# A two-block transformer kernel: 64 tokens of the expert stage computed from rows fetched by indirect DMA, the dense products 448 wide, query and key norms on ScalarE

## What is computed

```python
def one_block(hx):
    q = (hx @ w_q).reshape(TOKEN_BLOCK, PEER_HEADS, 2, PEER_HALF)
    s = jnp.einsum('nhpd,hpkd->nhpk', q, sub_keys).astype(jnp.float32)
    top_s, top_i = lax.top_k(s, PEER_TOPK)
    cand = top_s[:, :, 0, :, None] + top_s[:, :, 1, None, :]
    best_s, best_p = lax.top_k(cand.reshape(TOKEN_BLOCK, PEER_HEADS, PEER_TOPK * PEER_TOPK), PEER_TOPK)
    ...
    gate = jax.nn.softmax(best_s, axis=-1).reshape(TOKEN_BLOCK, PEER_HEADS * PEER_TOPK).astype(hx.dtype)
    u_sel = u[expert]
    v_sel = v[expert]
    act = jax.nn.gelu(jnp.einsum('nd,ned->ne', hx, u_sel), approximate=False)
    return jnp.einsum('ne,ned->nd', gate * act, v_sel)
```

## Time and profile before

| | |
|---|---|
| median of 3 runs | 2605.48 us |
| the profiled execution | 2603.68 us, its span 2601.9 us |
| TensorE matmul busy | 2467.9 us, 95% of the span |
| VectorE, ScalarE, GpSimd busy | 54%, 22%, 60% |
| TensorE clock granted, mean | 0.98 of full |
| DMA | 375.41 MB, mean 144 GB/s |

### The profile page before, as it was taken

How to read it: one execution, slowest core, us unless ns; L and a number is a source line. 1 busy time by engine, 2 the same in 40 slices (tenths; PEclk the granted TensorE clock), 3 DMA queues, 4 the chain that set the end, 5 groups by cost and what they waited for, 6 DMA issues and landing times.

```text
span 2601.9 us, 37796 instructions
## 1 busy us (share of the span) xinstructions
PE 2467.9 (95%) x12856; PEld 1258.8 (48%) x12856; DVE 1405.7 (54%) x2431; ACT 585.3 (22%) x1194; POOL 1559.2 (60%) x1048
## 2 busy tenths in 40 slices
PE   6879989999999999999999999999899898999997
PEld 3435534444555555434444444444357544457743
DVE  6996748998677777229722222240204533564434
ACT  2112211111222222111111111110126332245412
POOL 6764459888766766799866666560570166830063
PEclk8989999999999999999999999999999999999999
DMA  6224443555447857877755655560220022210021
GB/s 261 92 79 156 142 164 122 149 154 150 141 147 237 257 153 238 264 258 269 247 203 200 206 198 208 198 217 13 82 97 1 9 89 89 97 49 1 9 73 49
DMA packets 189247, 375.41 MB, mean 144 GB/s; under 512 B 13536, under 2 KB 79200, under 8 KB 189152
## 3 DMA queue, kind: packets, MB, share of 16 engines
q1 hardware_dynamic: 119696, 332.64, 38.2%
q10 hardware_dynamic: 69456, 41.50, 5.4%
HBM read 302.78 MB, written 71.30 MB: 144 GB/s over the span
## 4 chain that ended last, share of the span: by engine, by line
PE 83%; POOL 2%; DVE 2%; issue 1%; ACT 1%; DMA 0%; DVEq 0%; SPq 0%; POOLq 0%; ACTq 0%
PE ps L683 68%; PE ps L820 4%; PE ps L841 4%; PE ps L829 2%; PE ps L953 2%; PE ps L764 1%; POOL arena L653 1%; POOL parts L635 1%; DVE ps L1337 1%; ACT arena L1091 0%; POOL ring L633 0%; POOL arena L651 0%; DVE arena L1370 0%; PE ps L812 0%; PE ps L1053 0%
## 5 line engine op out<-in xcount | busy, mean ns | idle before, releaser
L683 PE MATMUL ps<-hT,parts 128*128 128x512 f16 x4800 | 1055.8, 380 | 38.2 <-DVE arena L1371 14.1
L632 POOL TENSOR_SCALAR parts<-ring 128x1024 f16<-128x1024 f32 x261 | 289.0, 1107 | 809.4 <-PE ps L683 784.1
L683 PEld LDWEIGHTS ps<-hT,parts 128*128 128x128 f16 x4800 | 467.0, 98 | 597.7 <-issue 22.3
L683 PE MATMUL ps<-arena 128*128 128x512 f16 x3072 | 667.4, 380 | 6.7 <-DVE arena L1734 6.7
L635 POOL TENSOR_TENSOR parts<-ring,parts 128x1024 f16<-128x1024 f32 x261 | 568.8, 2179 | 21.8
L683 PEld LDWEIGHTS ps<-arena 128*128 128x128 f16 x3072 | 301.2, 98 | 373.7 <-issue 14.8
L1729 DVE TENSOR_TENSOR arena<-arena 128x512 f32<-128x512 f32 x128 | 143.6, 1122 | 432.7 <-DMA arena<-gate_mem 430.2
L653 POOL TENSOR_TENSOR arena<-ring,arena 128x1024 f16<-128x1024 f32 x128 | 283.0, 2211 | 10.7
L633 POOL TENSOR_SCALAR ring<-ring 128x1024 f32<-128x1024 f32 x261 | 282.0, 1081 | 0.0
L651 POOL TENSOR_SCALAR arena<-ring 128x1024 f16<-128x1024 f32 x128 | 147.7, 1154 | 170.3 <-PE ps L683 170.3
L1202 ACT ACTIVATE spare<-ps 128x512 f32<-128x512 f32 x128 | 76.5, 597 | 567.5 <-PE ps L683 419.2
(11 more groups left out here) (172 smaller groups left out, 2270.2 us busy)
## 6 DMA issues: line engine op xcount, KB each, us to landing
ring<-w SPq DMA_DIRECT2D x133, 512.0 KB, 3.3
ring<-u SPq DMA_DIRECT2D x128, 512.0 KB, 3.9
ring<-v SPq DMA_DIRECT2D x128, 512.0 KB, 3.4
act_mem<-spare SPq DMA_DIRECT2D x128, 256.0 KB, 4.0
gate_mem<-arena ACTq DMA_DIRECT2D x4, 8192.0 KB, 42.7
arena<-act_mem SPq DMA_DIRECT2D x128, 256.0 KB, 3.6
arena<-gate_mem SPq DMA_DIRECT2D x128, 256.0 KB, 3.9
arena<-ada_w SPq DMA_DIRECT2D x48, 512.0 KB, 6.4
```

What stands on the lines that cost most here:

```text
L632: G.tensor_scalar(dst[:, 0, :], src, WS, 1.0, ALU.mult, ALU.mult).then_inc(scaled, 1)
L683: ins = [T.matmul(out_, a, b, start=start and j == 0, stop=stop and j == 2) for j, (a, b) in enumerate(((lhs[0], rhs[0]), (lhs[0], rhs[1]) ...
```

## The change

`FEW` = 64: the last 64 tokens leave the dense stage. `DENSE` = 448 tokens stay: up and down matmuls, gelu, `act_mem`, `gate_mem`, pairs and products are 448 wide; gates are spread in 56 groups (chunks 48 to 103), stored as 4 batches of 112 tokens (runs of 448 B). For the 64 tokens, expert numbers and gates go through a small HBM buffer (`pick_mem`) and come back with the 128 picks divided over two sides: partition 64h + n, column k holds pick 64h + k of token n. So one indirect DMA fetches 128 rows of 4 KB of `u` (or `v`), one per partition, into one of 4 buffers, and 64 of them make a pass. TensorE transposes the 64 tokens' features (32 matmuls), VectorE takes 64 dot products of 128x1024 with them out of PSUM, ScalarE applies gelu, and in the down stage VectorE adds 64 weighted rows of `v`; 8 fp32 matmuls with `fold` add the two sides.

GpSimd issues the fetches: 4 at chunk 56, then 3 ahead of each tile from chunk 108 on, then one at about every 1.75 chunks of the down stage. For tiles 108 to 127 of `u`, ScalarE does the first two of the three cutting operations. In the norms ScalarE squares out of PSUM and scales the keys and two of four query blocks; the gains are applied when the transposed rows are copied.

```diff
+            def cut_raised(n):
+                pool.wait_ge(raised, 2 * (n - T_EXP - RAISED + 1))
+                src, dst = ring[:, n % RING, :], parts[:, n % RING, :, :]
+                G.tensor_tensor(dst[:, 1, :], src, dst[:, 0, :], ALU.subtract).then_inc(parts_ready, 1)
+            def fetch(n):
+                if n >= ROWS_AHEAD:
+                    wait_apart(rows_used, n - ROWS_AHEAD + 1)
...
+                G.indirect_dma_start(
+                    out=fetched_rows[:, n % ROWS_AHEAD, :], out_offset=None, in_=rows,
...
-            cut_tiles(RING, T_TWO, 0)
+            cut_tiles(RING, T_EXP + FETCH, 0)
+            pool.wait_ge(pick_loaded, 16 * 2 * SIDES)
+            for n in range(ROWS_AHEAD):
+                fetch(n)
+            cut_tiles(T_EXP + FETCH, T_EXP + RAISED, 0)
+            n = ROWS_AHEAD
+            for c in range(RAISED, CHUNKS):
+                for _ in range(3):
+                    if n < FEW:
+                        fetch(n)
+                        n += 1
+                cut_raised(T_EXP + c)
+            while n < FEW + ROWS_AHEAD:
+                fetch(n)
+                n += 1
...
+            for c in range(CHUNKS):
+                while n < 2 * FEW and few_chunk(n - FEW) <= c:
+                    fetch(n)
+                    n += 1
                 cut_v(c)
...
-            ups(AT_GATES + 4, AT_GATES + S // GROUP, 4)
-            ups(AT_GATES + S // GROUP, CHUNKS)
+            ups(AT_GATES + 4, AT_GATES + GROUPS, 4)
+            for k in range(KC):
+                for side in range(SIDES):
+                    for j, half in enumerate(hr(k)):
+                        mm = T.matmul(ps[side * FEW:(side + 1) * FEW, 4 + k // 4, (k % 4) * P:(k % 4 + 1) * P],
+                                      half[:, DENSE:S], ident_h, start=(j == 0), stop=(j == 1))
+            mm.then_inc(few_turned, 1)
+            ups(AT_GATES + GROUPS, CHUNKS)
...
+            pe.wait_ge(rows_used, FEW)
...
+            for c in range(AT_GATES + GROUPS, CHUNKS):
+                gelu_chunk(c % 4, c)
+                if RAISED <= c + RING - 1 < CHUNKS:
+                    raise_tile(T_EXP + c + RING - 1)
...
+            for k in range(FEW):
+                row = await_rows(k)
+                V.tensor_tensor_reduce(out=row, in0=row, in1=few_h, scale=1.0, scalar=0.0, op0=ALU.mult,
+                                       op1=ALU.add, accum_out=few_dot[:, k:k + 1]).then_inc(rows_used, 1)
...
+                    V.scalar_tensor_tensor(out=few_sum, in0=row, scalar=w, in1=few_sum, op0=ALU.mult,
+                                           op1=ALU.add).then_inc(rows_used, 1)
```

```diff
-            take("q", lambda s, b: copy(tq[:, s, :], b))
-            take("kvi", lambda s, b: copy(tr[:, s, :], b[:, 0:KVI]))
+            for i in range(NT):
...
+                own.do(A.activation(mask[:, i, :], b, ACT.Square, scale=1.0 / WS), q_squares)
+                own.do(copy(tq[:, i, :], b), took["act"])
+            for i in range(NT):
...
+                for j, a in enumerate((0, 2 * HD)):
+                    own.do(A.activation(dup[:, j, i, 0:HD], b[:, a:a + HD], ACT.Square, scale=1.0 / WS,
+                                        accum_out=stat[:, i * 10 + 8 + j:i * 10 + 9 + j]))
+                own.do(copy(tr[:, i, :], b[:, 0:KVI]), took["act"])
...
+            for i in range(2, NT):
+                for h in range(HEADS):
+                    own.do(A.activation(tq[:, i, h * HD:(h + 1) * HD], tq[:, i, h * HD:(h + 1) * HD], ACT.Copy,
+                                        scale=stat2[:, i * 10 + h:i * 10 + h + 1]), tok_scaled)
```

More of the change, by code:

```diff
@@ L906, in _ @@
             features("up_attn", in_parts(oT), lambda k: pe.wait_ge(turned_read, 6 + k + 1))
-            features("out", in_parts(gT), lambda k: pe.wait_ge(tok_ready, 3 + k + 1), behind(1, 2))
+            features("out", in_parts(gT), lambda k: pe.wait_ge(tok_ready, 2 + k + 1), behind(1, 2))
             last_parts(1, 2)
@@ L938, in up @@
                 for k in range(KC):
-                    first, last = three(ps[:, r % 2, :], piece(T_EXP + r, k * P, P), hr(k), k == 0, k == KC - 1)
+                    hi, lo = hr(k)
+                    first, last = three(ps[:, r % 2, 0:DENSE], piece(T_EXP + r, k * P, P),
+                                        (hi[:, 0:DENSE], lo[:, 0:DENSE]), k == 0, k == KC - 1)
                     if k == 0:
@@ L992, in down_chunk @@
                     lhs, rhs = down_parts(at, o)
-                    first, last = three(ps[:, o, :], lhs, rhs, isinstance(c, int) and c == 0, False)
+                    first, last = three(ps[:, o, 0:DENSE], lhs, rhs, isinstance(c, int) and c == 0, False)
                 last.then_inc(down, 1)
@@ L1007, in _ @@
                     lhs, rhs = down_parts(c % (2 * GROUP), o)
-                    first, last = three(ps[:, o, :], lhs, rhs, False, c == CHUNKS - 1)
-                last.then_inc(down, 1)
+                    three(ps[:, o, 0:DENSE], lhs, rhs, False, c == CHUNKS - 1)
+                T.matmul(ps[:, o, DENSE:S], few_sum[:, o * P:(o + 1) * P], fold, start=True,
+                         stop=True).then_inc(down, 1)
                 if o >= 2:
@@ L1483, in _ @@
-            for i in range(NT):
-                dve.wait_ge(took["act"], count_taken("kvi", i))
-                own.do(V.tensor_tensor(scr[:, 0, 0:HD], tr[:, i, 0:HD], tr[:, i, 0:HD], ALU.mult))
-                own.link(V.tensor_tensor(scr[:, 0, HD:2 * HD], tr[:, i, 2 * HD:3 * HD], tr[:, i, 2 * HD:3 * HD], ALU.mult))
-                own.link(V.tensor_reduce(stat[:, i * 10 + 8:i * 10 + 10],
-                                         scr[:, 0, 0:2 * HD].rearrange("p (h d) -> p h d", d=HD), AX, ALU.add),
-                         stat_ready if i == NT - 1 else None)
@@ L1490, in _ @@
-            dve.wait_ge(root_ready, 1)
-            own.link(V.reciprocal(stat2[:, 0:40], stat2[:, 0:40]))
-            for i in range(NT):
+                dve.wait_ge(q_squares, i + 1)
+                own.do(V.tensor_reduce(stat[:, i * 10:i * 10 + 8], mask[:, i, :].rearrange("p (h d) -> p h d", d=HD),
+                                       AX, ALU.add), stat_ready if i == NT - 1 else None)
+            dve.wait_ge(root_ready, 1)
+            own.link(V.reciprocal(stat2[:, 0:40], stat2[:, 0:40]), rates)
@@ L1500, in _ @@
[L1500 to L1507 removed]
+                own.do(V.tensor_tensor(q3, q3, rs, ALU.mult), tok_ready)
```

221 lines of the change are left out of this document (149 added, 72 removed).

## The result

The changed kernel takes 2667.14 us (median of 4 runs, 2665.37 to 2671.51) against 2605.57 for the kernel before on the same chip: ratio 1.024, 95% interval 1.0228 to 1.0252. It is **slower by 61.6 us**; 2511 was forecast, with a range of 2470 to 2575.

A forecast was written before the change was run, and what follows sets the result against it. TensorE was taken as the bound, with DMA bounding the fetch phase and GpSimd the down stage after the change. Terms summed to -94.4 us from 2603.7, 2509.3, plus 1.8 for the median: 2511 us, range 2470 to 2575.

The forecast's parts named there:

- Norms: Start of the kernel: squares moved to ScalarE remove TensorE's wait for VectorE before the transposes, -3.4 us.
- Chunks 0 to 43: First up chunks: TensorE saves 11.1 us, then waits about 17 us for VectorE's gates; the exponentials wait for nothing new.
- The restart: Matmuls after TensorE's wait behind chunk 43 run partly at the lower clock level, +1.7 us.
- turning: Before the fetches: 32 TensorE matmuls that turn the 64 tokens' features, +2.1 us.
- folding: Down stage: eight fp32 matmuls adding the two sides, some 0.25 us each, +2 us.
- fetch phase: Chunk 104 to the end of up: DMA-bound at 400 GB/s, +34.9 us of waiting, +12.2 with narrower matmuls and fewer gates.
- the slower rival: Fetch phase and down: GpSimd's fetch costs more than 1.0 us; at 1.98 the whole gain is gone; 10%.
- Short runs: Gate stores: runs of 448 B might cost twice as much as 512 B, +40 us, 2551 us; 18%.
- The step that failed: Fetch phase: ScalarE's raising of tiles, some 2.2 us a chunk beside a gelu of 0.6, is hidden.
- signs of being wrong: Gate stage over 5.5 us a group, a fetch keeping GpSimd far from 1 us, or a fetch phase not DMA-bound.
- The down stage: Down chunks: GpSimd, busy 4.76 us a chunk, bounds the stage instead of TensorE at 4.545, -59.0 us.
- pause: Change from up to down: GpSimd's four fetches and cut take some 5 us, costing about what it did.

The follow-up runs named there:

- Experiment 1: Changed kernel with SyncE issuing each activation store before the load of a later tile, chunks 96 to 127: 2586.11 us (one run).
- 3: Changed kernel with GpSimd doing all three cutting operations and ScalarE no longer raising tiles, fetches kept: 2611.03 us (one run).
- 2: Changed kernel with 60 of the 64 fetches of `u` left out, dot products and ScalarE's raising kept: 2636.56 us (one run).
- experiment 4: Changed kernel with GpSimd issuing each fetch of `v` rows three chunks later in the down stage: 2625.54 us (one run).
- 5: Changed kernel with SyncE loading each chunk's pair ahead of the tile of `v` in the down stage: 2629.89 us (one run).
- kernel 6: Changed kernel with both SyncE's stores before loads (chunks 96 to 127) and `v` fetches three chunks later: 2545.45 us (median of 5), ratio 0.9775 to the kernel before.

## Why the prediction was wrong

**What held, and what held in part.** Norms: TensorE's products ended at 87.4, with 88.7 forecast (the kvi product moved the next one by 1.94 us, from 64.72 to 66.66, not by 3.1), the 6.52 us of wait went, and so did a restart that took 24 transposes 4.51 us instead of 2.78: the up stage starts 5.3 us earlier, 3.4 forecast. Chunks 0 to 43: -13.5 us against -14.5. The wait of some 17 us came, 16.1 of it, but in another place: 14.12 stand ahead of chunk 42, because ScalarE sat at the exponentials, 18.5 us, until VectorE's picks were there at 622.1, as before, with two gelus behind it. Before the change ScalarE came to the exponentials at 634.6 and waited for nothing. So "wait for nothing new" was right of their input and wrong of ScalarE, and what stood behind that wait was not followed: the same omission as below, here at no price. Gates: the period is 5.43 us as forecast. The restart cost 1.4 of 1.7 (24.04 us for five chunks, 22.68 at full speed), turning 1.0 of 2.1, folding 1.4 of 2.0 (no row stood behind its 0.25 us a matmul; it took 0.17, from 1852.78 to 1852.95). A fetch costs GpSimd 0.94 us in the fetch phase, 1.0 forecast: the slower rival, which needed 1.98, fell, and the kernel was slower for a reason that no case had.

**Short runs, a rival with 18%.** The four gate stores of the changed kernel are not alike. The second and third landed after 48.4 and 48.0 us, the first and last after 35.5 and 37.6; the four of before, 512 B a run, after 41.8 to 43.1. What the DMA engines were busy with them (packets, MB, share of 60 us from the issue), first the second store of before (870.6:930.6), then the first and second of the changed kernel (737.5:797.5 and 813.6:873.6):

```profile
q10 hardware_dynamic: 16400, 8.39, 48.7%
q10 hardware_dynamic: 16400, 7.34, 43.6%
q10 hardware_dynamic: 16400, 7.34, 56.8%
```

The third's share is 57.3%, the last's 43.4%. So a run of 448 B cost some 17% more than one of 512 B in two of the stores, and 10% less in the other two, which is near its part of the bytes. The stores differ in where in a row of 1792 B they begin (0, 448, 896, 1344 B); that this is the cause was not tried. Twice as much, as the rival had it, no store cost, and TensorE had no idle time in the gate stage; so the rival fell, but it was not without a ground. The Trainium skill has it, in DMA: Bandwidth & Descriptors, section "Specifications", that below 512 B a transfer is done as read-modify-write; the trace agrees for two stores of four, with a third more for each byte, and shows no such cost in the other two.

**The step that failed.** "Raising tiles on ScalarE, some 2.2 us a chunk beside a gelu of 0.6, is hidden too", with "GpSimd's share of a chunk is three fetches and 2.12 us". Both sums are right, as loads: ScalarE is busy 24.33 us of 114. Neither is a path. The raising was added to ScalarE's order behind a gelu, GpSimd's cut was made to wait for the raising, SyncE's load waits for the cut, the store is queued behind the load, and the next gelu but one waits for the store. The forecast asked how much each engine does in a chunk, and never followed what is queued behind each new wait; SyncE's queue, whose order was not changed, does not occur in that step at all. Price: 107.6 us where 12.2 were forecast, 95.4 too many. Experiment 1 cuts this loop at the store and 3 at the raising, and they give back 81 and 56 us; 2 takes the load off the DMA engines and leaves the loop, and gives back 31. One of the forecast's own signs of being wrong, a fetch phase not bound by DMA, is what came.

**The down stage.** "GpSimd: ... = 4.76 us" comes close to what the stage costs once its loop is cut, 4.81 measured. What was missed is the same thing again. GpSimd's fetch was taken as one microsecond of work and not as a wait for VectorE's row buffer, with the cutting behind it, the tile's load behind that, and VectorE's own pair behind the load. Price: -4.8 us in place of -57.

That 4.76 and 4.81 lie so near is in part luck. In experiment 4 the cutting took 3.68 us of GpSimd and the fetch 0.95, where 4.19 and 0.57 were forecast, and VectorE, "2.0 of 4.8, covered", had no slack. Over the same window (1460 to 1590 us) of experiments 4, 5 and 6 GpSimd was busy 124.93, 123.26 and 124.73 us of 130, and VectorE 128.91, 118.39 and 123.00, at 4.81 to 4.83 us a chunk each time: GpSimd's load is the steady one, as forecast, but part of it is time behind VectorE, and no experiment parts the two.

**What was off in size.** Kernel 6 has both loops cut and is the one to hold the sum against. It stands at 2545.5, 34.5 over the forecast, the result of three terms:

| stretch | kernel 6, us | change from before | forecast |
|---|---|---|---|
| to chunk 104 | 966.93 | -48.4 | -49.6 |
| fetch phase | 153.9 | +22.2 | +12.2 |
| pause | 15.7 | +13.2 | 0 |
| down | 628.5 | -46.4 | -57.0 |
| the rest | 777.8 | +0.3 | 0 |

Fetch phase: with the DMA engines full it moved 366 GB/s, not the 400 that the forecast took between 421 and 370 (kernel 6):

```profile
1005.00:1110.00 105.00, 84.13 (x375) 38.84 (x374) 57.09 (x93) 38.09 (x47) 75.61 (x62) 0.89 1.00 366
```

By that rate the forecast's 53.9 MB take 147.3 us instead of 134.7, 12.6 more; 10.0 are missing. Down: once in step, at 4.8 us a chunk, it is as forecast, but it starts badly, with a second pause of 7.54 us at 1160 for VectorE. The pause between up and down, 15.7 us where "some 5 us", as before, were forecast, is a third case of SyncE's order. Its timeline in kernel 6:

```profile
1119.11 1.06 POOL L706 TENSOR_SCALAR arena<-ring 128x1024 f16<-128x1024 f32 x1
...
1122.39 0.34 SPq L556 DMA_DIRECT2D ring<-v  x1
...
1127.03 0.42 SPq L607 DMA_DIRECT2D act_mem<-spare  x1
...
1132.52 0.54 ACT L1306 ACTIVATE spare<-ps 128x448 f32<-128x448 f32 x1 [12.70 <-DMA act_mem<-spare]
```

GpSimd cuts the first tiles of `v` only after four fetches of its rows, each of which waits for a dot product; the load of `v` waits for the cut; four pairs follow it; and the third last store of `act_mem` goes out behind them all at 1127.03, while the last gelu waits 12.70 us for stores. That this is worth mending was not tried.

## What to carry to other kernels

Beside the sum of each engine's work for one chunk, write down the cycle: from each new wait to what is queued behind it on the same engine or DMA queue, to who waits for that, until it closes; the longest cycle is the price, and it can be twice the largest load (experiment 2: 9.1 us, where the fullest engine, TensorE, had 4.54). When a window shows no resource near 1 and TensorE idle, look for such a cycle, and first at a queue where a transfer that frees something stands behind one that waits. Swapping two issues on SyncE was worth 81 us here, as much as the narrower products save in 125 chunks.

## What was not expected of the hardware

- **Stretched operations.** In experiment 4's down stage VectorE's 128x448 product (L1858) took 1.90 us on average, where its shortest took 0.61, and the sum over 128x1024 (L1870) 3.15, where its shortest in the changed kernel took 1.27. GpSimd's two operations went from 1.04 to 1.30 and from 2.12 to 2.38. In kernel 6 the second of these took 2.72 and VectorE's other product (L1856) 2.10: who pays differs from run to run. The Trainium skill says in SBUF — State Buffer, section "SBUF: two separate sides", that a VectorE operation with two SBUF inputs and a GpSimd operation that reads SBUF exclude each other for the whole instruction, whichever started first. The traces agree; two rows of kernel 6:

```profile
1501.36 2.98 POOL L708 TENSOR_TENSOR arena<-ring,arena 128x1024 f16<-128x1024 f32 x1
1502.28 2.54 DVE L1856 TENSOR_TENSOR arena<-arena 128x448 f32<-128x448 f32 x1
```

  The product, begun 0.9 us into GpSimd's operation, ended 0.48 us behind that operation's end. GpSimd's own 2.98 us had begun beside a sum of VectorE that ended at 1502.35.
- **A fetch has more than one price.** 0.94 us on GpSimd with VectorE at its dot products out of PSUM; beside the sums of the down stage 1.67 in experiment 4 and 1.21 in kernel 6. Issued back to back, one goes out every 1.25 us; in the changed kernel they landed after 6.2 us (`u`) and 5.3 (`v`).
- **The clock falls in the gaps.** In the changed kernel's fetch phase the 24 matmuls of a chunk took 6.00 to 7.67 us instead of 4.71 behind 17 of the 21 pauses (3.19 to 9.14 us long), and 4.71 behind the other four (1.40 to 3.23). The granted clock of the stretch was 0.78, between its two levels of 1.2 and 2.4 GHz. In the loop this cost nothing: the chunk begun at 1040.51 ended near 1046.5, and its gelu had still to wait for a store.
